# One decoder stage of a single-core kernel: delta rule heads started two tiles earlier, substitution in four parts, a new order in the recurrence, and transposes in place of small matmuls

## What is computed

```python
proj = h @ w_in                                   # q, k, v, z, beta_logit, a_logit
qkv = silu(causal_conv(qkv, w_conv))              # 4 taps
q = q * rsqrt(sum(q * q) + EPS) * d ** -0.5;  k = k * rsqrt(sum(k * k) + EPS)
beta = sigmoid(beta_logit);  g = -exp(a_log) * softplus(a_logit + dt_bias)
# per chunk of tokens (64 in the reference, 128 in the kernel) and head:
L = strict_lower(k_beta @ k.T * decay);  T = inverse(eye + L)
v_new = T @ v_beta - T @ (k_beta * exp(g_cum)) @ state
o = q_dec @ state + causal(q @ k.T * decay) @ v_new
state = state * exp(g_last) + k_dec.T @ v_new     # recurrence over the chunks
```

## Time and profile before

| what | us |
|---|---|
| device time, median of 3 runs | 2346.49 (2342.91 to 2348.24) |
| device time of the profiled execution | 2341.71 |
| its span, first to last instruction | 2339.9 |
| PE busy (matmuls) | 2211.8, 95% |
| DVE busy | 1127.8, 48% |
| ACT busy | 854.7, 37% |
| POOL busy | 412.3, 18% |

### The profile page before, as it was taken

How to read it: one execution, slowest core, us unless ns; L and a number is a source line. 1 busy time by engine, 2 the same in 40 slices (tenths; PEclk the granted TensorE clock), 3 DMA queues, 4 the chain that set the end, 5 groups by cost and what they waited for, 6 DMA issues and landing times. The chain is left out here.

```text
span 2339.9 us, 29203 instructions
## 1 busy us (share of the span) xinstructions
PE 2211.8 (95%) x10830; PEld 1776.7 (76%) x10830; DVE 1127.8 (48%) x1805; ACT 854.7 (37%) x1405; POOL 412.3 (18%) x459
## 2 busy tenths in 40 slices
PE   7999999999889999998899999999999997899989
PEld 6888887666677888887788878886777886776657
DVE  5444324423436444324575543346565775655433
ACT  4322223443334322223432241135445753433453
POOL 2111003112423111001210010002100241014441
PEclk8999999999989999999999999999999996999999
DMA  4333333411022333331333256740242220233202
GB/s 135 116 93 96 95 97 84 95 45 55 19 72 72 108 97 94 97 94 50 109 90 99 72 91 97 101 72 1 72 119 74 68 58 10 73 86 73 48 18 70
DMA packets 359321, 182.12 MB, mean 78 GB/s; under 512 B 41925, under 2 KB 356014, under 8 KB 358830
## 3 DMA queue, kind: packets, MB, share of 16 engines
q1 hardware_dynamic: 359214, 180.69, 31.0%
HBM read 176.14 MB, written 4.52 MB: 77 GB/s over the span
## 5 line engine op out<-in xcount | busy, mean ns | idle before, releaser
L313 PE MATMUL ps<-xh,wh 128*128 128x512 f32 x1920 | 766.0, 399 | 10.8 <-DVE wl L280 4.2
L315 PE MATMUL ps<-xh,wl 128*128 128x512 f32 x1920 | 749.3, 390 | 0.0
L314 PE MATMUL ps<-xl,wh 128*128 128x512 f32 x1920 | 748.5, 390 | 0.0
L280 DVE TENSOR_TENSOR wl<-raw,wh 128x1024 fp32r<-128x1024 f32 x334 | 422.6, 1266 | 435.7 <-ACT wh L270 431.0
L270 ACT ACTIVATE wh<-raw 128x1024 fp32r<-128x1024 f32 x334 | 342.1, 1027 | 375.3 <-PE ps L315 332.1
L313 PEld LDWEIGHTS ps<-xh,wh 128*128 128x128 f32 x1920 | 360.9, 188 | 102.9 <-issue 22.2
L315 PEld LDWEIGHTS ps<-xh,wl 128*128 128x128 f32 x1920 | 360.7, 188 | 77.3
L314 PEld LDWEIGHTS ps<-xl,wh 128*128 128x128 f32 x1920 | 361.1, 188 | 73.0 <-issue 2.4
L458 PE MATMUL ps<-xh,wh 128*128 128x512 f32 x304 | 129.9, 427 | 25.4 <-ACT xh L393 15.6
L451 POOL TENSOR_TENSOR acc<-acc,sq 128x512 f32<-128x512 f32 x72 | 102.6, 1424 | 273.1 <-ACT sq L836 178.0
L313 PE MATMUL ps<-a_hi,wh 128*128 128x512 f32 x352 | 136.9, 389 | 0.0
(11 more groups left out here) (380 smaller groups left out, 2560.7 us busy)
## 6 DMA issues: line engine op xcount, KB each, us to landing
raw<-in_w_ffn_gate SPq DMA_DIRECT2D x44, 512.0 KB, 3.8
raw<-in_w_ffn_up SPq DMA_DIRECT2D x44, 512.0 KB, 3.8
raw<-in_w_ffn_down SPq DMA_DIRECT2D x32, 512.0 KB, 3.8
raw<-in_conv_w_in SPq DMA_DIRECT2D x32, 512.0 KB, 4.0
raw<-in_fox_w_in SPq DMA_DIRECT2D x32, 512.0 KB, 9.9
raw<-in_gdn_w_in SPq DMA_DIRECT2D x32, 512.0 KB, 4.1
raw<-in_w_in SPq DMA_DIRECT2D x24, 512.0 KB, 3.8
raw<-in_swa_w_in SPq DMA_DIRECT2D x32, 256.0 KB, 3.8
```

Of the source, the lines that this page charges most:

```text
L280: nc.vector.tensor_tensor(wl[s][:, 0:kb, :], raw[r][:, 0:kb, :], wh[s][:, 0:kb, :].bitcast(F32), ALU.subtract).then_inc(lo_done, 1)
L313: pe.matmul(o, wh[s][:, kb, :], x_hi, start=start, stop=False)
L314: pe.matmul(o, wh[s][:, kb, :], x_lo, start=False, stop=False)
L315: return pe.matmul(o, wl[s][:, kb, :], x_hi, start=False, stop=stop)
```

## The change

Tile order: the narrow tile is number 4 now (BA = 4), k heads are tiles 0 to 3 and 5 to 8, q heads 9 to 16 as before. All gate steps move with it, five tiles' numbers counted from BA instead of from 8. K0 goes from 17 to 15, and the values are turned five tiles after their head's start (V_LAG) instead of three, so at the same tiles 20 to 27 as before; the last two in banks 2 and 4. Squares are summed one tile after they are made, k heads in bank 5, q heads one by one in bank 2, which the key transposes also use: each sum is added to EPS and copied by DVE (q_sums) before PE turns the next keys, and PE sums only after the keys are evicted (tok_d). All z tiles are evicted by ACT and POOL; substitution starts at step 25 in parts of 8, 8, 7 and 8 steps, and the three DVE instructions that turn the result back follow it in step 28; the ACT copies for the levels follow ACT's last eviction.

```diff
-        if k == H8:
+        if k == 4:
             return [(0, 2 * H8, v, 4 * D)]
-        if k < H8:
-            return [(0, P, v, D + k * P)]
...
-        m = pe.matmul(ps[STAT][:, t * P:t * P + P], rcol[:, t:t + 1].broadcast_to([P, P]), ident[:, :],
-                      start=True, stop=True)
+        m = pe.transpose(ps[STAT][:, t * P:t * P + P], rcol[:, t:t + 1].broadcast_to([P, P]), ident[:, :])
...
-            wait(pe, evac, ev0 + o - (3 if amid is None or first_i else 1))
+            wait(pe, evac, ev0 + o - (3 if amid is None or first_i or o in (4, 5) else 1))
...
-    K0, Z0, Z_POOL = 2 * H8 + 1, 3 * H8 + 1, 3 * H8 + 3
+    BA, K0, V_LAG, Z0 = 4, 2 * H8 - 1, 5, 3 * H8 + 1
...
-        if 3 <= k < 3 + H8:
-            square_of(act, 8 + k - 3, k - 3)
-        if 11 <= k < 11 + H8:
-            square_of(act, k - 11, H8 + k - 11)
+        if 3 <= k < 3 + 2 * H8:
+            square_of(act, (8 + k - 3) % 16, k - 3)
...
-        if k >= Z_POOL:
+        if k >= Z0:
             act.wait_ge(tile_done, t0 + k + 1)
             act.wait_ge(evac, ev0_ + k)
             nc.scalar.activation(G[:, k - 1, :], ps[two_banks(k)], ACT.Copy).then_inc(evac, 1)
+        if k == Z0 + H8 - 1:
+            act.wait_ge(tt_c, 1)
+            nc.scalar.activation(tt[32:64, :, 32:64], tt[32:64, :, 0:32], ACT.Copy).then_inc(tt_a, 1)
+            nc.scalar.activation(tt[64:96, :, 64:96], tt[64:96, :, 0:32], ACT.Copy).then_inc(tt_a, 1)
+            nc.scalar.activation(t11[32:64, :, 32:64], t11[32:64, :, 0:32], ACT.Copy).then_inc(t11_d, 1)
...
-        if s < 0 or s > H8 + 2:
+        if s < 0 or s >= H8 + V_LAG:
...
-            if s >= 3:
-                m = s - 3
+            if s >= V_LAG:
+                m = s - V_LAG
                 pe.wait_ge(c_silu, 2 * H8 + m + 1)
-                pe.wait_ge(qkt_d, m + 1)
+                pe.wait_ge(qkt_d, min(s - 2, H8))
+                if 0 < m < H8 - 2:
+                    pe.wait_ge(v_d, m)
+                if m == H8 - 1:
+                    pe.wait_ge(egc, H8)
+                    pe.wait_ge(dif, TB * H8)
+                if m == H8 - 2:
+                    pe.wait_ge(tok_d, H8)
                 for t in range(TB):
-                    ins = pe.transpose(blk(ps[3], t), blk(G[:, 16 + m, :], t), ident[:, :])
+                    ins = pe.transpose(blk(v_bank(m), t), blk(G[:, 16 + m, :], t), ident[:, :])
...
+                if k - 5 < 2 * H8:
+                    pe.wait_ge(q_sums, k - 4 - H8)
                 for t in range(TB):
                     ins = pe.transpose(blk(ps[2], t), blk(G[:, 8 + m, :], t), ident[:, :])
                 ins.then_inc(t_in, 1)
...
-        for turn in ([k - 4] if 4 <= k < 4 + H8 else []) + ([H8 + k - 11] if 11 <= k < 11 + H8 else []):
+        turn = k - 4
+        if 0 <= turn < 2 * H8:
             pe.wait_ge(g_sq, turn + 1)
-            if turn == 0:
-                pe.wait_ge(evac, ev0 + HEAD + 1)
-            bank, at_ = (ps[3], turn) if turn < H8 else (ps[7], turn - H8)
+            if turn == H8:
+                pe.wait_ge(evac, ev0 + HEAD)
+            bank, at_, apart = (ps[5], turn, H8) if turn < H8 else (ps[2], 0, 1)
+            if turn > H8:
+                pe.wait_ge(q_sums, turn - H8)
+            if k >= K0:
+                pe.wait_ge(tok_d, k - K0 + 1)
             for t in range(TB):
-                m = pe.matmul(bank[:, t * H8 + at_:t * H8 + at_ + 1], X[:, 11 + turn % 2, t * P:t * P + P], ones[:, 0:1],
+                m = pe.matmul(bank[:, t * apart + at_:t * apart + at_ + 1], X[:, 11 + turn % 2, t * P:t * P + P], ones[:, 0:1],
                               start=True, stop=True)
             m.then_inc(g_ss, 1)
-        if k == 13:
...
+        q = k - 4 - H8
+        if 0 <= q < H8:
+            dve.wait_ge(g_ss, H8 + q + 1)
+            nc.vector.tensor_scalar(nrm[:, 1, :, q:q + 1], ps[2][:, 0:TB].rearrange("p (t o) -> p t o", o=1),
+                                    EPS, None, ALU.add).then_inc(q_sums, 1)
...
+        if k == Z0:
+            g_tap(dve, k // 4, k % 4, 3)
...
-        if k == Z_POOL:
+        if k == Z0:
             dve.wait_ge(packed, TB * H8)
             dve.wait_ge(qd_p, H8)
             dve.wait_ge(pool_set, 2)
             link(dve, nc.vector.transpose(lc[:, :, :], cd[:, :, :].rearrange("p n i -> p i n")))
-            substitute(dve, 0, 10)
-        if k == Z_POOL + 1:
-            substitute(dve, 10, 20)
-        if k == Z_POOL + 2:
-            substitute(dve, 20, B5 - 1)
+            substitute(dve, 0, 8)
+        if k == Z0 + 1:
+            substitute(dve, 8, 16)
+        if k == Z0 + 2:
+            substitute(dve, 16, 23)
+        if k == Z0 + 3:
+            substitute(dve, 23, B5 - 1)
+            nc.vector.transpose(t11[:, :, 0:B5].rearrange("p n c -> p c n"),
+                                ti[:, :, :].rearrange("p i c -> p c i")).then_inc(t11_d, 1)
+            nc.vector.transpose(tt[:, :, 0:B5].rearrange("p n i -> p i n"), ti[:, :, :]).then_inc(tt_c, 1)
+            dve.wait_ge(tt_c, 1)
+            nc.vector.tensor_copy(tt[96:128, :, 96:128], tt[96:128, :, 0:32]).then_inc(tt_a, 1)
+
+    def v_bank(m):
+
+        return ps[3] if m < H8 - 2 else ps[2] if m == H8 - 2 else ps[4]
 
...
+                for r in range(NR if t else 0):
+                    m = NR * rd + r
+                    pe.wait_ge(o_tok, at(rd, t - 1, r))
+                    pe.wait_ge(qd_p, m + 1)
+                    pe.matmul(ps[4 + r][:, 0:P], blk(G[:, m, :], t), blk(state, r), start=True, stop=False)
+                for r in range(NR if t < TB - 1 else 0):
+                    pe.wait_ge(vn_d, at(rd, t, r))
+                    if t == 0:
+                        pe.wait_ge(*((back_a, 2 * H8 + 2 * rd + r + 1) if r < 2 else (tok_d, H8 + 2 * rd + r - 1)))
+                    pe.matmul(ps[r][:, 2 * P:3 * P], kdec(r, t), blk(vnew, r), start=True, stop=True).then_inc(s_mm, 1)
                 for r in range(NR):
                     m = NR * rd + r
                     pe.wait_ge(vn_d, at(rd, t, r))
                     if t == 0:
-                        pe.wait_ge(*((back_a, 2 * H8 + 2 * rd + r + 1) if r < 2 else (tok_d, H8 + 2 * rd + r - 1)))
-                    if t < TB - 1:
-                        pe.matmul(ps[r][:, 2 * P:3 * P], kdec(r, t), blk(vnew, r), start=True, stop=True).then_inc(s_mm, 1)
-                    if t:
-                        pe.wait_ge(o_tok, at(rd, t - 1, r))
-                        pe.wait_ge(qd_p, m + 1)
-                        pe.matmul(ps[4 + r][:, 0:P], blk(G[:, m, :], t), blk(state, r), start=True, stop=False)
-                    else:
                         pe.wait_ge(qkt_m, m + 1)
                     pe.matmul(ps[4 + r][:, 0:P], blk(qkt(m), t), blk(vnew, r), start=t == 0, stop=True).then_inc(o_mm, 1)
 
     def dve_tail(dve, ev0_):
-        nc.vector.transpose(t11[:, :, 0:B5].rearrange("p n c -> p c n"),
-                            ti[:, :, :].rearrange("p i c -> p c i")).then_inc(t11_d, 1)
...
-                for r in range(NR if t else 0):
+            for t in range(TB + 1):
+                for r in range(NR if 0 < t < TB else 0):
                     m = NR * rd + r
                     dve.wait_ge(ks_mm, at3(rd, t - 1, r))
                     nc.vector.scalar_tensor_tensor(out=blk(rest_, r), in0=ps[r][:, 0:P], scalar=tab[:, BEGC, t, m:m + 1],
                                                    in1=blk(G[:, 16 + m, :], t), op0=ALU.mult, op1=ALU.subtract).then_inc(r_d, 1)
+                for r in range(NR if t else 0):
+                    m = NR * rd + r
+                    dve.wait_ge(o_mm, at(rd, t - 1, r))
+                    nc.vector.tensor_copy(blk(G[:, m, :], t - 1), ps[4 + r][:, 0:P]).then_inc(o_tok, 1)
                 for r in range(NR if t < TB - 1 else 0):
                     m = NR * rd + r
                     dve.wait_ge(s_mm, at3(rd, t, r))
                     if t:
-                        dve.wait_ge(o_mm, at(rd, t, r))
                         nc.vector.scalar_tensor_tensor(out=blk(state, r), in0=blk(state, r), scalar=tab[:, EGL, t, m:m + 1],
                                                        in1=ps[r][:, 2 * P:3 * P], op0=ALU.mult, op1=ALU.add).then_inc(s_d, 1)
                     else:
                         if rd:
                             dve.wait_ge(o_mm, at(rd - 1, TB - 1, r))
                         nc.vector.tensor_copy(blk(state, r), ps[r][:, 2 * P:3 * P]).then_inc(s_d, 1)
-                for r in range(NR):
-                    m = NR * rd + r
-                    dve.wait_ge(o_mm, at(rd, t, r))
-                    nc.vector.tensor_copy(blk(G[:, m, :], t), ps[4 + r][:, 0:P]).then_inc(o_tok, 1)
 
     def act_tail(act, ev0_):
-        silu_of_z(act, Z0 + H8 - 1)
-        act.wait_ge(tt_c, 1)
-        nc.scalar.activation(tt[32:64, :, 32:64], tt[32:64, :, 0:32], ACT.Copy).then_inc(tt_a, 1)
         act.wait_ge(kk_mm, 2 * H8 + 1)
         act.wait_ge(qd_p, H8)
```

(39 more changed lines are left out.)

54 lines of the change are left out of this document (24 added, 30 removed).

## The result

| kernel | median, us | lowest to highest | runs |
|---|---|---|---|
| before | 2346.49 | 2339.69 to 2348.86 | 5 |
| changed | 2328.86 | 2326.15 to 2328.99 | 5 |

The ratio is 0.9926, 95% interval 0.991 to 0.9942: 17.4 us less (13.6 to 21.1). A second comparison gave 0.9931 (0.9917 to 0.9946). The forecast was 2329.0.

A forecast was written before the change was run, and what follows sets the result against it. PE was taken as the bound inside tiles, its waits as the other cost. Second level 7.2, recurrence 4.2, spreads 5.5 and mix_in 0.7 sum to 17.6 us, giving 2329.0 from the median; own range 2323 to 2335, with A and B 2316 to 2339.

The forecast's parts named there:

- The wait moves ahead of tile 32: End of gdn_in: PE's wait for the substitution does not vanish but becomes 8.8 us, 1.7 at tile 31, 7.1 at tile 32.
- Second level 7.2 us earlier: Levels after gdn_in's tiles: second level at 1951.2 instead of 1958.35 us, all gains up to there included; bounds 4.5 to 9.3.
- Start 4.6: Start of gdn_in, tiles 3 to 6: tile 4 needs one eviction instead of three; 4.6 us gained.
- Gate chain 3.0: Gate constants in gdn_in move from step 11 to 7, so PE's wait for a square behind tile 12 goes: 3.0 us.
- Recurrence 4.2: Recurrence: the new instruction order takes chunks from 5.50 to 4.7 us, 4.2 us in all; bounds 2.0 to 5.6.
- Spreads 5.5: Eleven spreads and the L1585 groups, transposes instead of matmuls: 0.45 us per spread at full clock, 5.5 summed; bounds 2.5 to 7.
- mix_in 0.7: Tile 4 of mix_in: PE's wait of 0.94 us goes, worth 0.7 us; bounds 0 and 0.9.
- A: Rival at tile 32: the substitution holds nothing, second level gains 17.9 us instead of 7.2; total 2318 us, chance 0.15.
- B: Rival: early gains are eaten, by DVE setting some tiles or a longer stretch at 1.2 GHz; total 2336 us, chance 0.22.
- C: Rival in tiles 16 to 20: q sums and key transposes share bank 2, PE waits for DVE; total 2351 us, chance 0.04.
- D: Rival: transposes hold PE at 1.2 GHz after spreads, six inside heads costing 15 us; total 2344 us, chance 0.04.
- E: Rival: the change does not do what it says, another engine sets all early tiles; no change, 2343 us, chance 0.05.

## Why the prediction was right

- **The wait moves ahead of tile 32**: shown. Forecast 8.8 us in two pieces (1.7 and 7.1), measured 6.6 (0.4 and 6.2); split 32 was done 46.6 us after tile 24's end, not 48.2. The term that was over by 1.6 us is the substitution: 29.4 us were read off the trace of before and 27.7 were taken, one of POOL's multiplications fewer beside it. Tile 32 to the first level took 8.7 us for 8.25. The errors partly cancel.
- **Second level 7.2 us earlier**: 11.15, of which the sums and waits ahead of tile 3 gave 3.7; 0.45 for the head's spread belongs to my 7.2, so 7.9 stand against 7.2.
- **Start 4.6**: 4.4 measured, and 4.4 lost when undone. **Gate chain 3.0**: tile 5 to 17 gained 1.8 against the trace of before (80.30 for 82.13), and 3.5 against those of the kernels with only the wait or only the order changed (83.8), in which 3.4 us at the lower clock fall into this stretch. These lie just behind the chain's wait of 2.7 us (at 1791.8 and 1794.8), four of the five traces with the old chain have them or more, and none of the nine with the new one. So 1.8 is the gain without the clock and 3.5 the gain with it; only the first is under the 3.0 forecast.
- **Recurrence 4.2**: 4.3 in the trace, 4.0 alone in the runs (5.5 in the trace of that run); the chunk 4.61 for 4.7.
- **Spreads 5.5**: mis-sized, on the spot 7.7 in the kernel before, 6.7 for the spreads and 1.0 for L1585; in the runs 3.3 to 4.6 when undone in the changed kernel, 1.2 when made alone. Transposes last 0.35 for 0.81; the factor of 2.3 stands against the four of the Trainium skill ("TensorE: Matmul & The Clock Gate", Terms), so the row was right to decide.
- **mix_in 0.7**: its wait is gone, 0.9 us.
- **Rivals.** A: the wait is there, so no. B: in the heads no tile waits for DVE beyond 0.8. C: no q sum and no key transpose waits for DVE; the only waits for it in the heads are two at the q·k of a head (L2253), 1.2 us in all, where the kernel before had one of 0.7. D: not in the heads, where 1820 to 1910 us has clock 1.00 with transposes in each tile, and not in the mean clock. The Trainium skill ("TensorE: Matmul & The Clock Gate", Part 4: PE-mode transpose) says that a transpose does not count as PE busy in the same way; no run here shows a lower clock that comes from it. E: no; its 2343 does not follow either, since no change against the median is 2346.5.

The span fell by 12.6 and the median by 17.4, and this is no contradiction: the profiled execution of before was one of its quick ones (2341.71, 4.8 under its median), that of the changed kernel lay at its median (2328.99). Taking the sum off the median, as I did, was the right choice.

That 2328.86 lies 0.14 us from 2329.0 is luck. What the terms show on the spot is 7.9 + 4.3 + 7.3 + 0.9 = 20.4 us (7.3 is 7.7 less the head's spread, which is in the 7.9), against 17.6 forecast, and the two comparisons gave 17.4 and 16.2. The forecast had no term for what the clock took elsewhere: in the traces 10.2 us more at the lower clock ahead of tile 3, by 0.43 each an estimated 4.4 us, and 1.8 behind the recurrence. The spreads were put too low, and the two errors cancel.

## What to carry to other kernels

Lay out a long chain on a helper engine around the short pieces for which the bound engine waits: here 4.7 us of turned values ahead of a 1.2 us split cost 7 us, part of it through the clock that falls in the wait. Moving one piece behind the other gained more on PE than any stretch of the table above (4.9 at most). Judge an edit of under 5 us by its own stretch in the trace, between two marks that it does not touch, and then by undoing it in the full kernel; the span of one execution differs by 13 us for the same program (2337.3 to 2350.8 in the 73 runs of the kernel before). And look beside a long chain for work of a third engine that makes its instructions longer, here POOL's.

## What the runs showed of the hardware

- The same instructions, on at least three chips: up to 20.5 us more or less at 1.2 GHz in 1720 us (88.7 to 109.2), and 8.9 us between the quickest and the slowest. It is not the chip alone: on one chip 33 runs of the kernel before have mean clocks from 0.961 to 0.968.
- Time at the lower clock costs 0.43 us per us up to tile 3 and about 0.35 behind the recurrence, not 0.5: part of it falls where PE waits anyhow (in the changed kernel PE is idle in 32 of the 102 us ahead of tile 3).
- Small edits shift a kernel's mean clock, with no transposes involved too: 0.9627 over 12 runs with only a wait loosened, 0.9646 over the 33 of before beside them. At 0.9615 such a shift hid the 7.7 us of the spreads almost wholly. Why was not found.
- An instruction of VectorE's substitution that meets a multiplication on POOL lasts 0.9 to 1.5 us instead of 0.2 to 0.45, 14 times of 14 in three traces.
